# Empty tiles ahead of the split operands of a three-product matmul kernel

## The reference

```python
# first block
h = _layer_norm(ALPHA * h + 0.5 * _swiglu(h, ffn1_w_gate, ffn1_w_up, ffn1_w_down), ...)   # d_ff 2816
mix = _token_mixers(h, w_in, ...)            # gated recurrence + spatial gating, then @ w_out
h = _layer_norm(ALPHA * h + mix, ...)
xa = _memory_cross_attention(h, mem, ...)    # 256 memory tokens, wq, wk, wv, wo
h = _layer_norm(ALPHA * h + xa, ...)
h = _layer_norm(ALPHA * h + 0.5 * _swiglu(h, ffn2_w_gate, ffn2_w_up, ffn2_w_down), ...)
# second block
z = modulate(h, c) @ w_in                    # 1024 -> 8704
m = ga * (ya @ w_out_a) + gb * (yb @ w_out_b) + gc * (yc @ w_out_c)
out = h + gate * (m @ w_o)
```

## Time and profile before

| | us |
|---|---|
| median of three runs | 1708.55 |
| profiled execution, first to last instruction (span) | 1706.6 |
| TensorE busy (matmuls) | 1691.5 |
| TensorE busy (weight loads, beside the matmuls) | 1394.7 |
| VectorE busy | 994.7 |
| ScalarE busy | 683.6 |
| GpSimd busy | 166.8 |

### The profile page before, as it was taken

One profiled execution on the slowest core, in us unless ns is written; L12 is line 12 of the kernel. 1 busy time (PEld: TensorE's weight loads), 2 busy tenths in 40 slices (PEclk: granted clock), 3 DMA queues, 4 the chain that ended last, 5 costly groups with the idle time before them and its releaser, 6 DMA issues.

```text
span 1706.6 us, 22901 instructions
## 1 busy us (share of the span) xinstructions
PE 1691.5 (99%) x8500; PEld 1394.7 (82%) x8500; DVE 994.7 (58%) x1341; ACT 683.6 (40%) x975; POOL 166.8 (10%) x158
## 2 busy tenths in 40 slices
PE   9999999999999999999999999999999999999999
PEld 7888888888787888888888888877778787788887
DVE  5333339987965784666333333457976869844442
ACT  4222232246454465434222223346454445732330
POOL 0000000112004521013000000013011020000000
DMA  5333247633122353223332233323333222243331
GB/s 216 98 98 98 91 138 231 222 121 119 52 98 66 109 182 137 67 82 123 98 98 94 92 130 117 109 87 118 85 99 95 86 83 86 74 123 109 104 109 62
DMA packets 51476, 188.05 MB, mean 110 GB/s; under 512 B 5776, under 2 KB 6288, under 8 KB 50512
## 3 DMA queue, kind: packets, MB, share of 16 engines
q1 hardware_dynamic: 44640, 161.50, 29.7%
q10 hardware_dynamic: 5184, 16.00, 2.9%
q0 software_dynamic: 1584, 9.60, 1.6%
HBM read 182.89 MB, written 4.19 MB: 110 GB/s over the span
## 4 chain that ended last, share of the span: by engine, by line
PE 89%; DVE 7%; ACT 2%; issue 1%; DMA 0%; POOL 0%; SPq 0%; DVEq 0%; ACTq 0%; POOLq 0%
PE proj L422 83%; DVE w_lo L414 1%; PE aux L1859 1%; PE aux L1846 1%; PE aux L1619 1%; PE aux L1836 1%; DVE y L2016 0%; ACT w_hi L407 0%; DVE score L1221 0%; DVE qk L1264 0%; DVE md L1242 0%; PE aux L566 0%; DVE qk L1265 0%; PE aux L1839 0%; DVE md L1241 0%
## 5 line engine op out<-in xcount | busy, mean ns | idle before, releaser
L414 DVE TENSOR_TENSOR w_lo<-raw,w_hi 128x1024 fp32r<-128x1024 f32 x300 | 380.5, 1270 | 388.8 <-ACT w_hi L407 382.0
L422 PE MATMUL proj<-a_hi,w_hi 128*128 128x512 f32 (+1 forms) x1536 | 600.8, 391 | 3.3 <-DVE a_lo L909 1.8
L422 PE MATMUL proj<-a_hi,w_lo 128*128 128x512 f32 (+1 forms) x1536 | 591.3, 385 | 0.0
L422 PE MATMUL proj<-a_lo,w_hi 128*128 128x512 f32 (+1 forms) x1536 | 591.0, 385 | 0.0
L407 ACT ACTIVATE w_hi<-raw 128x1024 fp32r<-128x1024 f32 x300 | 315.3, 1053 | 233.4 <-PE proj L422 164.3
L422 PEld LDWEIGHTS proj<-a_hi,w_hi 128*128 128x128 f32 x1536 | 288.5, 188 | 67.9 <-issue 5.8
L422 PEld LDWEIGHTS proj<-a_lo,w_hi 128*128 128x128 f32 x1536 | 288.7, 188 | 58.4 <-issue 2.9
L422 PEld LDWEIGHTS proj<-a_hi,w_lo 128*128 128x128 f32 x1536 | 288.5, 188 | 58.5
L422 PE MATMUL proj<-hid_hi,w_hi 128*128 128x512 f32 (+1 forms) x374 | 142.6, 381 | 0.0
L422 PE MATMUL proj<-hid_hi,w_lo 128*128 128x512 f32 (+1 forms) x374 | 140.9, 377 | 0.0
L422 PE MATMUL proj<-hid_lo,w_hi 128*128 128x512 f32 (+1 forms) x374 | 140.8, 377 | 0.0
(11 more groups left out here) (368 smaller groups left out, 2011.1 us busy)
## 6 DMA issues: line engine op xcount, KB each, us to landing
raw<-stream SPq DMA_DIRECT2D x303, 512.0 KB, 3.5
ctxk<-ada_in ACTq DMA_DIRECT2D x12, 512.0 KB, 3.7
ctxv<-ada_in ACTq DMA_DIRECT2D x12, 512.0 KB, 3.9
out<-h ACTq DMA_DIRECT2D x7, 256.0 KB, 2.0
h<-x_in SPq DMA_DIRECT2D x3, 512.0 KB, 8.7
btab<-rpb_in POOLq DMA_DIRECT2D x4, 384.0 KB, 3.5
cond_row<-cond_in ACTq DMA_DIRECT2D x1, 1024.0 KB, 5.9
side<-mem_in POOLq DMA_DIRECT2D x1, 1024.0 KB, 5.2
```

Source lines behind the costliest of these rows:

```text
L414: nc.vector.tensor_tensor(w_lo[:, st.slot], raw[:, st.slot], w_hi[:, st.slot].bitcast(F32), ALU.subtract).then_inc(lo_ready, 1)
L422: mm = nc.tensor.matmul(dst, a, b, start=start and n == 0, stop=stop and n == 2)
```

## The change

Seven empty tiles are added, which nothing writes or reads. They take 64, 128 or 192 bytes per partition each. No instruction is added, removed or moved: on each of the five engines the instructions stand in the same order with the same operands and the same waits, and only the operands' places in SBUF differ. (The lines behind the new ones get numbers higher by 1 to 7, so L422 of the kernel before is L423 of the changed one.)

```diff
         w_lo = sb("w_lo", [P, RING, SB * P], F32R)
+        sb("past_the_weights", [P, 48])
         h = sb("h", [P, KD, T])
...
+            sb("before_hid_hi", [P, 16], F32, ph)
             hid_hi = sb("hid_hi", [P, KF, T], F32R, ph)
+            sb("before_hid_lo", [P, 16], F32, ph)
             hid_lo = sb("hid_lo", [P, KF, T], F32R, ph)
...
             side = sb("side", [P, KD, M], F32, ph)
+            sb("before_side_hi", [P, 48], F32, ph)
             side_hi = sb("side_hi", [P, KD, M], F32R, ph)
+            sb("before_side_lo", [P, 16], F32, ph)
             side_lo = sb("side_lo", [P, KD, M], F32R, ph)
...
+            sb("before_m_hi", [P, 32], F32, ph)
             m_hi = sb("m_hi", [P, KD, T], F32R, ph)
+            sb("before_m_lo", [P, 48], F32, ph)
             m_lo = sb("m_lo", [P, KD, T], F32R, ph)
```

## The result

The changed kernel takes 1740.98 us, median of four runs (1740.83 to 1741.27), against 1708.28 us beside it (1707.91 to 1709.06): a ratio of 1.019, 95% interval 1.0176 to 1.0205. The forecast was 1670. The time went where rival 4 said it would if it went up: into the pitch of the three-product matmuls.

The account below looks back on a forecast made before the run. TensorE's three-product matmuls were taken to bound the kernel. Gains of 32.0 and 12.3 us make 44.3, of which 92%, 40.8, counts; about 2 us off leaves 38.5 less: 1670 us, range 1650 to 1690.

Parts of the forecast that it names:

- rival 4: Slower: at the new distance 512-column matmuls of L422 meet the weight load worse, one more 6.67 ns step, 1749 us; chance 0.06.
- What bounds the kernel: TensorE's three-product matmuls at L422, 83% of the chain that ended last; their pitch times their number is most of the time.
- 92%: Share of a gain on L422 expected to reach the end: 44.3 us of TensorE's time becomes 40.8 us.
- That `ctx_*` is faster because of its distance: At 256 columns `ctx_*`, 192 bytes from the weights modulo 512, loses 6.7 ns per matmul; the others, at 0, lose 13.3.
- Rival 1: The place of the operands doesn't matter and `ctx_*` is faster for another reason; time 1708.5 us, chance 0.10.
- 512 columns behave as 256 do: Assumption for `a_*` and `mix_*` moved to distance 192: 6.67 ns saved per matmul, 32.0 us together.
- 4800 matmuls priced at -6.67 ns: `a_*` moving (4608) and `mix_*` (192), put at distance 192: 32.0 us less of TensorE's time.
- The unknown distances: `hid_*`, `side_*`, `m_hi`, moving weights and `xpt_*`, 1842 matmuls at distances no row shows: the same 6.67 ns gain, 12.3 us.
- The controls named in advance: In the merge `y_*` must stay at 226.7 ns; `a_*` staying at 226.7 would show everything wrong.

## Why the prediction was wrong

- **What bounds the kernel** was right. The time moved with the pitch of L422 and with nothing else; TensorE's waits stayed. 94% of the change of TensorE's time arrived, where I had reckoned with 92%.
- **That `ctx_*` is faster because of its distance** was right too: moved to 128 it lost 5.1 ns, `a_*` moved to 192 gained 5.9 ns in its 256-column matmuls, and the run with everything moved together excludes the starting place. Rival 1 has fallen. So has what I drew from the rule that I held against the reading, that the places of the two operands could not matter: the Trainium skill's pages "TensorE: Matmul & The Clock Gate" (section "Step-by-step: what each phase is for") and "SBUF — State Buffer" (section "Who interferes with whom") have loading take nothing from a running matmul and TensorE wait on nobody, and here the same instructions took 32.7 us longer at other places.
- **The step that failed** is the one from 256 to 512 columns, "What I take over here is that 512 columns behave as 256 do". The reason I gave was that the loss at distance 0 is the same for both widths, from which I had concluded that it "belongs to the change of weights, once for each matmul". The equality is true and says nothing on other distances: at 192 the loss is 6.7 ns for 256 columns and 20.0 ns for 512. Of the 4800 matmuls priced at -6.67 ns, the 192 of 256 columns came out as forecast, at -5.9 ns; the 4608 of 512 columns cost +6.3 ns (`a_*`) and +5.9 ns (`mix_*`), the size of the step nearly right and its sign wrong. 96 matmuls of one width were the whole evidence for 4608 of another, and the sentence "no row shows 512 columns at any other distance than 0" stood in the text, at the rival that came true, with a chance of 0.06.
- **The unknown distances.** "One of two distances seen is bad and that one is the special one" turned out upside down. At 512 columns distance 0 is the special one because it is the best of the twelve tried, and 256 is as good as 0; the moved tiles of the changed kernel were at 229 ns or more. The 12.3 us of gain that I took for them in full were -0.4 us at 256 columns, as forecast in sign, and +5.1 (`hid_*`), +1.1 (`m_*`) and +0.9 us (moving weights) at 512.
- **A rule that I did not think of**: `hid_*` at 256 and 320 and `m_*` at 320 and 0 lie at unlike distances within a chain. Put right for `hid_*`, this took its pitch from 232.0 to 226.9 ns, and the kernel was 4.2 us faster.
- **The range** (1650 to 1690) left rival 4 out on purpose. Its price, one more step of 6.67 ns for all moved tiles, was 1749; the time came out at 1741, because the moved tiles gained at 256 columns, the 240 matmuls in which weights move over `a_*` lost only 1.2 ns, and `a_*` and `hid_*` lost 6.3 and 5.2 ns and not 6.67.
- The controls named in advance served: `y_*` stayed within 0.5 ns (226.8 to 227.3), and `a_*` in the second network told the verdict in one row.

## What to carry to other kernels

Where weight load and matmul alternate without a pause, the places of the two operands in SBUF were worth 2% of this kernel's time, and a small tile added between them can change that time without touching an instruction. For these three-product matmuls at 512 columns it paid to start all moving operands where the weights start, modulo 256 bytes; at 256 columns a distance of 192 was better. Look at the pitch, not the duration alone, after a change of the layout. A natural experiment in a trace carries over only to what is alike in all that matters; before a measured difference is multiplied by thousands, ask which of the two cases the thousands are, here the width. When the only row is of the other kind, the opposite sign deserves more than a leftover chance.

## What the runs showed of the hardware

In these kernels the three-product matmuls never reach the time of their columns, 213.3 ns for 512 at the granted clock of 1.00 (2.4 GHz): the best mean pitch is 226.7. In steady rows at distance 0 the loss is 13.3 ns for 256, 384 and 512 columns. At distance 192 it is 6.7 ns at 256 columns, 13.3 at 320, 13.3 to 16.7 at 384 and 20.0 at 512. At 512 columns it depends on the distance of moving from loaded operand modulo 256 bytes and hardly on a common move of both (1.0003).

A steady row has a repeating pattern: 226 and 227 ns at distance 0; 236, 231, 236, 231, 236, 230 for `a_*` in the changed kernel, with the mean 233.3. And a row takes a while to become steady, which the sums above don't show. In the kernel before, 423 of 5973 pitches of 512 columns over a fixed weight block lie above 227 ns, mostly at 228 to 236, although all are at distance 0. 372 of them are among the first eleven matmuls behind a pause or behind other work of TensorE. In the changed kernel 5592 of 5980 lie above 227, and most of the others are those of `y_*`, still at distance 0. So distance 0 does not spare the loss from the start: such a row as a rule falls into the pattern of 226.7 ns within its first eleven matmuls or so and stays in it, and at 192 it stays at 233.3. Why is not shown. That the two reads meet in parts of the memory that repeat every 256 bytes would fit the period, but no run shows such parts, and the runs with half loads and the several levels at one distance do not fit a simple count of meetings.
